# Gate and up products of a gated feed-forward stage with the input's high and low part as one 512-column operand

## The reference

```python
def swiglu(h, w_gu, w_down):
    gu = jnp.einsum('bsd,df->bsf', h, w_gu)
    g, up = gu[..., :D_FF], gu[..., D_FF:]
    return jnp.einsum('bsf,fd->bsd', jax.nn.silu(g) * up, w_down)
```

## Time and profile before

| what | value |
|---|---|
| median of 3 runs | 1237.8 us (1237.79 to 1237.91) |
| profiled execution | 1238.25 us, its span 1236.6 us |
| TensorE busy | 1176.8 us, 95% of the span |
| VectorE busy | 813.1 us, 66% |
| ScalarE busy | 559.6 us, 45% |
| mean granted TensorE clock | 0.98 of full speed |

### The profile page before, as it was taken

One profiled execution on the slowest core, in us unless ns is written; L12 is line 12 of the kernel. 1 busy time (PEld: TensorE's weight loads), 2 busy tenths in 40 slices (PEclk: granted clock), 3 DMA queues, 4 the chain that ended last, 5 costly groups with the idle time before them and its releaser, 6 DMA issues.

```text
span 1236.6 us, 20207 instructions
## 1 busy us (share of the span) xinstructions
PE 1176.8 (95%) x8020; PEld 1079.1 (87%) x8020; DVE 813.1 (66%) x1040; ACT 559.6 (45%) x650; POOL 115.2 (9%) x99
## 2 busy tenths in 40 slices
PE   5989899999998989999969999998999998999997
PEld 4878899999787889999959999987989997999996
DVE  6466857786857685778686677767468377444444
ACT  4464443433447544343334343444695445433432
POOL 3300600000240060000010000000000000000000
PEclk9989999999899999999979999999999999999999
DMA  9612377766271237676636567753423543554540
GB/s 362 224 68 103 136 284 277 280 260 257 85 256 69 103 137 288 272 284 259 254 106 235 201 254 291 281 212 137 170 103 137 186 160 145 202 194 172 201 170 35
DMA packets 34851, 242.68 MB, mean 196 GB/s; under 512 B 3792, under 2 KB 5216, under 8 KB 8176
## 3 DMA queue, kind: packets, MB, share of 16 engines
q1 hardware_dynamic: 27792, 196.03, 42.9%
q0 software_dynamic: 5520, 45.17, 10.0%
q10 hardware_dynamic: 1488, 0.76, 0.2%
HBM read 240.90 MB, written 1.05 MB: 196 GB/s over the span
## 4 chain that ended last, share of the span: by engine, by line
PE 77%; DVE 12%; ACT 5%; issue 4%; DMA 1%; SPq 0%; POOL 0%; DVEq 0%; ACTq 0%
PE bank L418 73%; ACT w_hi L802 2%; DVE x_lo L1187 2%; DVE w_lo L1114 2%; DVE work L1230 1%; PE bank L493 1%; DVE small L1130 1%; DVE x_hi L1185 1%; DMA raw<-stream 1%; PE bank L581 1%; DVE h L1143 1%; DVE h L1163 1%; PE bank L571 1%; DVE z L1159 1%; PE bank L558 1%
## 5 line engine op out<-in xcount | busy, mean ns | idle before, releaser
L1114 DVE TENSOR_TENSOR w_lo<-raw,w_hi 128x2048 fp32r<-128x2048 f32 x184 | 432.3, 2356 | 231.1 <-ACT w_hi L802 231.0
L418 PE MATMUL bank<-x_hi,w_hi 128*128 128x256 f32 x1824 | 520.8, 286 | 4.0 <-DVE w_lo L1114 1.8
L418 PE MATMUL bank<-x_lo,w_hi 128*128 128x256 f32 x1824 | 516.9, 283 | 0.0
L418 PE MATMUL bank<-x_hi,w_lo 128*128 128x256 f32 x1824 | 516.7, 283 | 0.0
L802 ACT ACTIVATE w_hi<-raw 128x2048 fp32r<-128x2048 f32 x184 | 350.8, 1908 | 180.5 <-PE bank L418 174.8
L418 PEld LDWEIGHTS bank<-x_hi,w_hi 128*128 128x128 f32 x1824 | 350.9, 192 | 10.8 <-issue 4.8
L418 PEld LDWEIGHTS bank<-x_lo,w_hi 128*128 128x128 f32 x1824 | 350.9, 192 | 1.8
L418 PEld LDWEIGHTS bank<-x_hi,w_lo 128*128 128x128 f32 x1824 | 350.7, 192 | 0.0
L418 PE MATMUL bank<-w_hi,hid_hi 128*128 128x512 f32 x352 | 139.3, 396 | 2.1 <-DVE hid_lo L1218 2.1
L418 PE MATMUL bank<-w_lo,hid_hi 128*128 128x512 f32 x352 | 139.0, 395 | 0.0
L418 PE MATMUL bank<-w_hi,hid_lo 128*128 128x512 f32 x352 | 139.0, 395 | 0.0
(11 more groups left out here) (162 smaller groups left out, 1125.3 us busy)
## 6 DMA issues: line engine op xcount, KB each, us to landing
raw<-stream SPq DMA_DIRECT2D x184, 1024.0 KB, 4.8
work<-ada POOLq DMA_DIRECT2D x24, 1536.0 KB, 7.6
gain_rows<-rows POOLq DMA_DIRECT2D x11, 512.0 KB, 6.5
gate_rows<-rows POOLq DMA_DIRECT2D x3, 512.0 KB, 11.0
h<-x SPq DMA_DIRECT2D x4, 256.0 KB, 4.9
out<-z SPq DMA_DIRECT2D x4, 256.0 KB, 2.1
c<-consts SPq DMA_DIRECT2D x1, 962.0 KB, 12.7
wf<-w_f ACTq DMA_DIRECT2D x2, 256.0 KB, 12.7
```

The lines of the kernel that those rows point to most:

```text
L418: last = nc.tensor.matmul(out, stationary, moving, start=start and i == 0, stop=stop and i == 2, skip_group_check=True)
L1114: nc.vector.tensor_tensor(w_lo[j % SLOTS][:, :], raw[j % SLOTS][:, :], w_hi[j % SLOTS][:, :].bitcast(F32), ALU.subtract).then_inc(lo_ready, 1)
```

## The change

The parts x_hi and x_lo become the two halves of one tile x_parts, so that for each k they lie side by side as 512 columns. In the gate and up chunks of the feed-forward stages the two matmuls with w_hi (on x_hi and on x_lo) become one matmul of 512 columns that fills a whole bank: its first 256 columns hold w_hi*x_hi, the last 256 hold w_hi*x_lo. The matmul w_lo*x_hi stays one of 256 columns, onto the first half. Each half n has a bank of its own now (gate: banks 0 and 1, up: banks 2 and 3), and the two halves of a bank are added afterwards: ScalarE copies the second halves to SBUF, VectorE adds the first halves. All other products stay as they are.

```diff
+        x_parts = sb("x_parts", [P, KT, 2, S], F32R)
+        x_hi, x_lo = x_parts[:, :, 0, :], x_parts[:, :, 1, :]
...
+        gate_rest = view(2 * S)
+        up_sum = view(2 * S)
...
+        GATE, UP = banks[:, 0:2, :], banks[:, 2:4, :]
...
+            def split_projection(t, j, pair, before=lambda k: None):
+                pe.wait_ge(lo_ready, 3 * t + (j + 1))
+                wh, wl = chunk(w_hi, j % SLOTS, KT), chunk(w_lo, j % SLOTS, KT)
+                for k in range(KT):
+                    before(k)
+                    for n in range(2):
+                        cols = slice(n * P, (n + 1) * P)
+                        nc.tensor.matmul(pair[:, n, :], wh[:, k, cols], x_parts[:, k, :, :].rearrange("p a n -> p (a n)"),
+                                         start=k == 0, stop=False, skip_group_check=True)
+                        last = nc.tensor.matmul(pair[:, n, 0:S], wl[:, k, cols], x_hi[:, k, :], start=False,
+                                                stop=k == KT - 1, skip_group_check=True)
+                last.then_inc(chunk_done, 1)
...
                 def gate_up(t, j, i):
-                    pe.wait_ge(silu_done, FT * f + i)
-                    projection(t, j, B[0], x_hi, x_lo)
-                    pe.wait_ge(hidden_ready, FT * f + i)
-                    projection(t, j + 1, B[1], x_hi, x_lo)
+                    pe.wait_ge(gate_ready, FT * f + i)
+                    split_projection(t, j, GATE)
+                    pe.wait_ge(up_ready, FT * f + i)
+                    split_projection(t, j + 1, UP)
...
-                pe.wait_ge(silu_done, FT * f + FT)
+                pe.wait_ge(gate_ready, FT * f + FT)
+                pe.wait_ge(up_ready, FT * f + FT)
...
                 def step(t, j, n):
-                    after_gate(t, j, n)
+                    gate_rest_out(t, j)
                     split(t, j + 3)
+                    silu(n)
+                    up_rest_out(t, j, n)
                     split(t, j + 4)
                     act.wait_ge(chunk_done, 3 * t + (j + 3))
                     hidden_hi(n)
                     split(t, j + 5)
...
+                def gate_summed(n):
+                    dve.wait_ge(gate_rest_kept, n + 1)
+                    rest = gate_rest.rearrange("p (a n) -> p a n", a=2)
+                    nc.vector.tensor_tensor(rest, GATE[:, :, 0:S], rest, ALU.add).then_inc(gate_ready, 1)
+
+                def after_up(n, first=False):
+                    dve.wait_ge(up_rest_kept, n + 1)
+                    rest = up_sum.rearrange("p (a n) -> p a n", a=2)
+                    nc.vector.tensor_tensor(rest, UP[:, :, 0:S], rest, ALU.add).then_inc(up_ready, 1)
+                    dve.wait_ge(up_ready, n + 1)
                     dve.wait_ge(silu_done, n + 1)
                     if not first:
                         dve.wait_ge(hid_ready, n)
-                    nc.vector.tensor_tensor(hidden, gate_act, B[1][:, :], ALU.mult).then_inc(hidden_ready, 1)
+                    nc.vector.tensor_tensor(hidden, gate_act, up_sum, ALU.mult).then_inc(hidden_ready, 1)
...
                 def step(t, j, n, i):
+                    gate_summed(n)
                     split(t, j + 3)
-                    after_up(t, j, n)
+                    after_up(n)
                     split(t, j + 4)
```

More of the change, by code:

```diff
@@ L94, in fused_blocks @@
         x_full = sb("x_full", [P, 4, S])
-        x_hi = sb("x_hi", [P, KT, S], F32R)
-        x_lo = sb("x_lo", [P, KT, S], F32R)
+        x_parts = sb("x_parts", [P, KT, 2, S], F32R)
+        x_hi, x_lo = x_parts[:, :, 0, :], x_parts[:, :, 1, :]
         mix_hi = sb("mix_hi", [P, KT, S], F32R)
@@ L132, in fused_blocks @@
         attn_end = used[0]
+        used[0] = attn_end + KT * ADA_COLS
+        gate_rest = view(2 * S)
+        up_sum = view(2 * S)
+        used[0] = attn_end
         u_s = view(2 * ATT).rearrange("p (m n) -> p m n", m=2)
@@ L176, in fused_blocks @@
         out_scale = small[:, 128:130]
-        B = [ctx.enter_context(nc.psum_tensor(f"bank{i}", [P, 512], F32)) for i in range(8)]
+        banks = ctx.enter_context(nc.psum_tensor("bank", [P, 8, 512], F32))
+        B = [banks[:, i, :] for i in range(8)]
+        GATE, UP = banks[:, 0:2, :], banks[:, 2:4, :]
         RES = B[4:8]
@@ L226, in fused_blocks @@
         out_scale_ready = sem("out_scale_ready")
+        gate_rest_kept = sem("gate_rest_kept")
+        gate_ready = sem("gate_ready")
+        up_rest_kept = sem("up_rest_kept")
+        up_ready = sem("up_ready")
         silu_done = sem("silu_done")
@@ L506, in gate_up @@
                 def gate_up(t, j, i):
-                    pe.wait_ge(silu_done, FT * f + i)
-                    projection(t, j, B[0], x_hi, x_lo)
-                    pe.wait_ge(hidden_ready, FT * f + i)
-                    projection(t, j + 1, B[1], x_hi, x_lo)
-                projection(t, j, B[0], x_hi, x_lo, before=input_tile(n_in))
-                projection(t, j + 1, B[1], x_hi, x_lo)
+                    pe.wait_ge(gate_ready, FT * f + i)
+                    split_projection(t, j, GATE)
+                    pe.wait_ge(up_ready, FT * f + i)
+                    split_projection(t, j + 1, UP)
+                split_projection(t, j, GATE, before=input_tile(n_in))
+                split_projection(t, j + 1, UP)
                 gate_up(t, j + 2, 1)
@@ L823, in ffn, with hidden_hi @@
             def ffn(t, j, f, with_ada, final=False):
-                def after_gate(t, j, step, first=False):
+                def gate_rest_out(t, j):
                     act.wait_ge(chunk_done, 3 * t + (j + 1))
-                    if not first:
-                        act.wait_ge(hidden_ready, step)
-                    nc.scalar.activation(gate_act, B[0][:, :], ACT.Silu).then_inc(silu_done, 1)
-                def hidden_hi(step, out=hid_hi):
-                    act.wait_ge(hidden_ready, step + 1)
+                    nc.scalar.activation(gate_rest.rearrange("p (a n) -> p a n", a=2), GATE[:, :, S:2 * S], ACT.Copy)\
[9 more added lines that the diff above has]
+                        .then_inc(up_rest_kept, 1)
+                def hidden_hi(n, out=hid_hi):
+                    act.wait_ge(hidden_ready, n + 1)
                     nc.scalar.activation(out[:, :, :].rearrange("p k n -> p (k n)"), hidden, ACT.Copy)\
@@ L841, in step @@
                     split(t, j + 5)
-                after_gate(t, j, FT * f, first=True)
+                gate_rest_out(t, j)
                 split(t, j + 3)
+                act.wait_ge(gate_ready, FT * f + 1)
+                nc.scalar.activation(gate_act, gate_rest, ACT.Silu).then_inc(silu_done, 1)
+                act.wait_ge(chunk_done, 3 * t + (j + 2))
+                nc.scalar.activation(up_sum.rearrange("p (a n) -> p a n", a=2), UP[:, :, S:2 * S], ACT.Copy)\
+                    .then_inc(up_rest_kept, 1)
                 split(t, j + 4)
                 hidden_hi(FT * f)
-                after_gate(t, j + 2, FT * f + 1)
+                gate_rest_out(t, j + 2)
                 split(t, j + 5)
+                silu(FT * f + 1)
+                up_rest_out(t, j + 2, FT * f + 1)
                 split(t, j + 6)
@@ L859, in ffn @@
                                          ada_acc[:, SHIFT_SCALE * P:], ACT.Copy).then_inc(acc_hi_ready, 1)
-                after_gate(t, j + 5, FT * f + (FT - 1))
+                gate_rest_out(t, j + 5)
                 split(t, j + 8)
+                silu(FT * f + (FT - 1))
+                up_rest_out(t, j + 5, FT * f + (FT - 1))
                 hidden_hi(FT * f + (FT - 1), hid_hi2)
```

11 lines of the change are left out of this document (6 added, 5 removed).

## The result

The changed kernel takes 1229.7 us in the median of 5 runs (1228.0 to 1233.3), the kernel before 1237.8. The ratio is 0.9943, with a 95% interval of 0.9928 to 0.9957: 0.57% faster, some 7 us. The forecast was 1223.5, with a gain of 14.3: the time lies inside the stated range of 1220 to 1233.5 and the direction is right, but the gain is only about half of what was forecast (0.57% of 1237.8 are 7.1 us). The profiled execution took 1229.68 us, its span 1228.0.

The account below looks back on a forecast made before the run. The prediction took TensorE's matmuls to bound the kernel: 78 chunks saving 0.211 us give 16.5, less 2.1 for stage ends, so 14.4 off 1238.25, then 0.45 lower for the median: 1223.5 us. Range of 8 in 10: 1220 to 1233.5.

Parts of the forecast that it names:

- What bounds the kernel: Inside a feed-forward stage a nanosecond less on TensorE is one less in the time, while VectorE, at 72%, has room.
- The pair then takes 346.5 ns and saves 13.2: Gate and up chunks: three 256-column matmuls (359.7 ns) become one of 512 and one of 256; a chunk saves 0.211 us.
- Rival 1: Long matmul costs 233.3 ns as in the down chunk: 6.0 us less in all, 1231.8 us; chance 0.14.
- The prediction's own sign for it: In the changed kernel's timeline, a loop step of 16.9 us would show Rival 1 right; the forecast had 16.69.
- The fixed part seems to go with the stationary operand: Gate and up chunks: ground for pricing the long matmul at the mixer's 226.6 ns, with w_hi stationary, not 233.3.
- The Trainium skill's fixed part: About 2.5 ns per warm back-to-back matmul; by it a chunk saves 0.04 us, total about 1237; set aside for the trace's 13.
- Which chunks count: Of 88 gate and up chunks 78 count: 19 in each of stages 1 to 3, 21 in stage 4; 16.5 us.
- The added work: ScalarE copies and VectorE sums cost nothing in the loop; the up sum costs 0.69 us at three stage ends, 2.1 us.
- The wait of sum_gates for up_ready: End of stages 1 to 3: this new wait ends at about 622.6, and its four matmuls finish before hid_lo does.
- rival 2: With x moving, the fixed part goes with the columns: 239.8 ns for 512; only the tail's 2.1 us left, 1239.9; chance 0.06.
- Rival 3: Turns of long and short matmuls break TensorE's flow, 113 ns 8 times a chunk: 56 us more, 1294; chance 0.05.
- Rival 4: VectorE falls behind in the loop of stages 1 to 3, needing 16.9 us a step: 8.5 us less gain, 1232; chance 0.07.

Follow-up runs that it names:

- Run 2: Changed kernel with the short matmul made 512 columns too (w_lo on both parts), so all matmuls of the gate and up chunks are long: 1359.8 us, ratio 1.0995.
- run 1: Changed kernel with the 16 long matmuls of a gate or up chunk first and its 16 short ones behind them: 1226.7 us, ratio 0.9913.
- run 12: Run 8 with only the w_lo tiles moved to 32 bytes past a multiple of 128: 1222.1 us, ratio 0.9879 to the kernel before.
- run 4: Kernel before with 32 bytes of padding ahead of the hid tiles, which puts them at a multiple of 128 bytes: 1233.5 us, ratio 0.9965.
- run 13: run 11 with 32 more bytes ahead of hid, so w, x and hid all begin 32 bytes past a multiple of 128: 1232.4 us, ratio 0.9956.
- run 9: Kernel before with 96 bytes of padding ahead of the hid tiles, which puts them 64 bytes past a multiple of 128: 1236.6 us, ratio 0.9999.
- run 11: Kernel before with 32 bytes of padding ahead of all its tiles: 1237.1 us, ratio 0.9992.
- run 10: Kernel before with x_hi, x_lo, mix_hi and mix_lo moved off by 32 bytes, hid as before: 1226.2 us, ratio 0.9909.
- run 5: Changed kernel with the order long, long, short, short for each k in the place of long, short, long, short: 1225.2 us, ratio 0.9898.
- run 3: Changed kernel with its long matmul as two of 256 columns again; copies, sums, waits and bank pairs stay: 1238.7 us, ratio 1.0019 to the kernel before.
- Run 8: run 7 with mix_lo placed behind the up sum and the product at the end of stages 1 to 3: 1213.6 us, ratio 0.9808 to the kernel before.
- run 7: Changed kernel with long matmuls first in the gate chunk, short first in the up chunk, and hid tiles aligned: 1218.2 us, ratio 0.9842.
- run 6: Changed kernel with the 32 bytes of padding ahead of the hid tiles that run 4 has: 1225.7 us, ratio 0.9900.

## Why the prediction was right in its places and wrong in its size

**What bounds the kernel: right.** TensorE has no wait from up0 to down8, and each change of its pace in runs 1 to 13 came back as time.

**The term that failed: "The pair then takes 346.5 ns and saves 13.2".** It was made of two prices, each read from a stretch of like matmuls: 119.9 ns for 256 columns and 226.6 for 512. Both are right for such stretches. Run 2 shows 226.7 for the long ones with this very pair of operands, and run 1 has 119.9 for the short ones. The pair in turn takes 352.8, 6.3 ns more than their sum of 346.5, and this the trace of before could not show, since no stretch of it has the lengths in turn. So the step that failed is the addition: that the price of a mixture is the sum of the prices of its parts. Run 1 shows that the order is the cause; whether the two lengths or the two writes to one bank make it is open. The chunk saves 0.110 us and not 0.211, 78 chunks 8.6 and not 16.5; with the stage ends that is 6.7 us.

**Rival 1** gave 1231.8, close to what came out, by the wrong mechanism: it took the down chunk's 233 ns for the price of 512 columns in this stage. Run 2 refutes it. The prediction's own sign for it, a loop step of 16.9 us, came true (16.88), so that sign could not tell the two causes apart; that the time lies inside the range is owed to it too, and is luck as far as the cause goes. Number and cause have to be held apart here: a pair of 352.8 ns alone looks like 233 + 120, and only a stream of long ones could tell.

**"The fixed part seems to go with the stationary operand": wrong as put.** It goes with the pair, and in run 12 not even with that alone. Hid lay at 96 bytes past a multiple of 128 and w at 0; with both at 0 (run 4) or both at 32 (run 13) the 233 ns become 227, with hid at 64 (run 9) or w at 32 and hid at 0 (run 11) they don't. The value that I chose by it, 226.6 for w with x, was right, because these two begin at the same offset.

**The Trainium skill's fixed part** of about 2.5 ns per warm matmul ("TensorE: Matmul & The Clock Gate", section "Wait — 56ns, not 53.3ns?") does not show here. The smallest in a stream of like matmuls is 10.1 ns (116.8 for 256 columns, run 10), the usual 13.2; single intervals behind a long matmul go down to 112 ns (run 5), still 5.3 above 106.7.

**Which chunks count: right.** Gate0 gains nothing, since up0 begins when its w_lo is made; gate10 and up10 of stages 1 to 3 gain nothing. Stage 4 gained 2.03 us from down0 on.

**The added work: right.** Nothing in the loop (run 3), 0.64 us at each of three ends where 0.69 was forecast, 2.3 us in all by run 3. The wait of sum_gates for up_ready was there and covered. Run 8 took 0.54 us a stage back by moving mix_lo out of that chain.

**Rivals 2 to 4:** 512 columns with x moving cost 226.7 and not 239.8 (run 2), so rival 2 is out. Rival 3 looked at the right place, the turn of long and short matmuls, and at the wrong price: it had 113 ns at each of 8 breaks, 0.90 us a chunk, where 6.3 ns at each of 16 pairs came, 0.10 us. A change of banks by itself breaks nothing (runs 2 and 3). Rival 4 is out: the sums take 0.69 us each and VectorE is at 81%.

## What to carry to other kernels

A price per matmul read from a stretch of equal matmuls holds for such a stretch; when an edit mixes lengths, test the mixture, and put matmuls of one length together where the accumulation lets you choose the order. Compare the offsets of stationary and moving tile within 128 bytes: in a stream of 512-column matmuls equal offsets saved 6.7 ns each, while for 256 columns unequal ones saved 3.1, and a few words of padding moved the time by 0.35 to 0.9%. Measure it with the whole kernel: moving w_lo alone (run 12) made the time some 0.7% longer, by way of matmuls whose own tiles had stayed. Where the end of a stage has another bound than its loop, read its chain by itself: an instruction that costs nothing in the loop was paid in full there.

## What the runs showed of the hardware that was not expected

At the 2.4 GHz level, with 128 x 128 stationary tiles in fp32r, the distance between starts was:

| moving columns | offsets of the two tiles within 128 bytes | ns | runs |
|---|---|---|---|
| 256 | equal (0 and 0; 32 and 32) | 119.9 | before, 3, 4, 11, 13 |
| 256 | unequal (w 0, x 32) | 116.8 | 10 |
| 512 | equal (0 and 0; 32 and 32) | 226.7 | before (mixer), 2, 4, 7, 13 |
| 512 | equal, but w_lo of the step at 32 | 232 | 12 |
| 512 | unequal (96 and 0; 64 and 0; 0 and 32) | 233 to 234 | before, 9, 11 |
| 512 and 256 in turn | equal | 352.8 a pair | after, 6 |
| two of 512, two of 256 in turn | equal | 696 for the four | 5 |

A stream of equal 512-column matmuls that follows shorter ones or a wait takes five to ten intervals of 224 to 241 ns before it is even (5 in run 7, 7 in the gate chunk of run 1, 9 in run 6, 10 behind the first one of down10 in run 4). Why equal offsets help long matmuls and hurt short ones, why run 12's long ones lose the even pace, and why the strict turn costs 6.3 ns a pair and the double turn 1.5, stays open: the runs show the conditions and not the mechanism.
